# Expert loop of a mixture-of-experts block: weights split into two halves against plain f32 with the weights stationary and one ring of buffers

## The chip, the cores and the metric

The kernel runs on one core of one Trainium2 chip. The metric is the device time of the core in microseconds (us); less is better. The kernel before has a median of 4677.69 us over three runs.

## The reference, cut to what matters

The program computes two transformer blocks. The change touches one part of the first, the expert-choice feed-forward: each of 16 experts takes its 64 tokens of 512 (`cap` = 2 x 512 / 16), with D = 1024 and an inner width F = 2048, in float32.

```python
def expert_choice_ffn(h, w_router, w_gate, w_up, w_down):
    B, N, D = h.shape
    cap = EC_FACTOR * N // N_EXPERTS
    aff = jax.nn.softmax((h @ w_router).astype(F32), axis=-1)
    gate, idx = lax.top_k(jnp.swapaxes(aff, 1, 2), cap)
    xg = jax.vmap(lambda hb, ib: hb[ib])(h, idx)
    hid = jax.nn.silu(jnp.einsum('becd,edf->becf', xg, w_gate)) * jnp.einsum('becd,edf->becf', xg, w_up)
    y = jnp.einsum('becf,efd->becd', hid, w_down) * gate[..., None].astype(h.dtype)
    return jax.vmap(lambda yb, ib: jnp.zeros((N, D), yb.dtype).at[ib.reshape(-1)].add(yb.reshape(-1, D)))(y, idx)
```

The three weight tensors hold 16 x 3 x 1024 x 2048 x 4 bytes = 402.65 MB, and each byte is used once.

## The kernel before, in words

The program runs its stages one after another: modulation, norm, mixers, output projection, then `route` (the router, the choice of tokens, and the chosen tokens gathered into `ex_xg`, feature-major), `weights_back` (the weighted one-hot matrices `ex_back` that carry an expert pair's rows back to the tokens), `expert_loop`, a last norm (`final_sq` and so on), and the whole second block. Only `expert_loop` and the layout of its weights change.

`expert_loop` handles the experts in pairs: 8 turns of `positions`, each of 32 positions; the first seven turns are a hardware loop over one body, the last is written out. A position handles one chunk of 128 inner features of one expert: 16 chunks an expert, 256 in all. The work of a chunk is spread over several positions (`has(LEAD)`, `has(2)`, `has(1)`, `has(0)`):

- SyncE loads a 1 MB tile of gate and up weights (`ex_gu`, L1735) and a 0.5 MB tile of down weights (`ex_d`, L1740), four buffers each.
- Each weight tile is split into two halves of type float32r, high and low, which TensorE streams faster than plain float32. ScalarE casts the high halves (L1812, L1823), VectorE subtracts for the low half of gate and up (L1876), GpSimd for that of down (L1841).
- TensorE keeps the tokens stationary (`ex_xe`, 64 tokens as high and low part, 128 columns) and streams the 256 weight columns: 16 matmuls a chunk (L1770), then two plain f32 matmuls of 128 columns that add the token halves and turn the result (`ex_raw`, L1780).
- VectorE copies `ex_raw` out of PSUM (L1882), multiplies by the SiLU that ScalarE made (L1888), and splits the product into `ex_hT` (L1892, L1894). TensorE then streams the down weights with `ex_hT` stationary: 4 matmuls of 512 columns a chunk (L1794).
- At the end of an expert the two halves of the result are added into `ex_y` (L1828, L1904). Eight plain f32 matmuls a pair (L1757) carry the rows back to the 512 tokens, and VectorE adds them to `x` (L1860).

A plain f32 matmul of the program stands in the trace as two records, each a weight load (LDWEIGHTS, "PEld") and a MATMUL; one with float32r operands stands as one. Numbers of records are halved for plain f32 wherever instructions are meant.

## Time and profile before

| what | value |
|---|---|
| median of 3 runs (lowest, highest) | 4677.69 us (4676.04, 4678.01) |
| profiled execution: span from first to last instruction | 4676.2 us |
| mean granted TensorE clock, as a share of full speed | 0.878 |
| `expert_loop`, from its first weight load issued to its last add | 1214.2 to 2631.2 us, so 1417.0 us |
| DMA over the whole span | 573.07 MB, mean 123 GB/s |

The page prints no time of the profiled execution beside its span; the span lies between the lowest run and 1.5 us under the median, so nothing of weight lies around it. Engines are PE (TensorE matmul), PEld (its weight loads), DVE (VectorE), ACT (ScalarE), POOL (GpSimd), SP (SyncE). In the views by stretch each engine has its busy time, with the number of its instructions in brackets; PEclk is the granted clock, where 1.00 is 2.4 GHz and 0.50 is 1.2 GHz. A matmul's busy time includes its way through the pipeline, so the rate of a stream is read from the distance between starts, not from the duration of a record.

### The profile page before, as it was taken

The page shows a single profiled execution, that of the slowest core. Times are in us where ns is not written, and L with a number is a line of the kernel's source. Part 1 is how long each engine was busy: PE and PEld are TensorE (multiplying, and loading weights), DVE is VectorE, ACT ScalarE, POOL GpSimd, SP SyncE. Part 2 cuts the span into 40 slices and gives each one's busy share as a digit, 9 for nine tenths or more (in the row PEclk, how much of TensorE's full clock was granted, in tenths as well). Part 3 has the DMA queues.
Part 4 walks back from the last instruction along what each step waited for, and adds up shares of the span by engine and source line. Part 5 has one row for each costly group of instructions (what it writes and reads, how often), then busy time and mean ns, then how long its engine had stood idle before and what let it go on. Part 6 is the DMA issues. An engine that isn't in the chain of part 4 may idle for free. (4 is left out here: it accounts for less than half of the span.)

```text
span 4676.2 us, 54928 instructions
## 1 busy us (share of the span) xinstructions
PE 3468.8 (74%) x18716; PEld 2774.4 (59%) x18716; DVE 2909.6 (62%) x4362; ACT 1528.0 (33%) x1968; POOL 1362.9 (29%) x512
## 2 busy tenths in 40 slices
PE   6683767876777777777777676877676987877968
PEld 3473537865565666666656345757355865766856
DVE  5224647773799998999999645349747823144441
ACT  5110421112355555555555431112013521212121
POOL 0020000001255555655555202115320033333423
PEclk9895888967899999999999888887788998988989
DMA  6110000000587887887887531000010022222322
GB/s 250 50 61 9 5 25 1 1 15 23 214 296 270 299 295 273 297 294 273 298 296 281 190 117 50 35 26 1 0 45 7 1 72 72 73 71 77 98 66 74
DMA packets 136745, 573.07 MB, mean 123 GB/s; under 512 B 12977, under 2 KB 17457, under 8 KB 103729
## 3 DMA queue, kind: packets, MB, share of 16 engines
q1 hardware_dynamic: 136528, 570.21, 34.4%
q8 instruction: 132, 2.16, 0.2%
q14 instruction: 85, 0.70, 0.0%
HBM read 568.07 MB, written 2.10 MB: 122 GB/s over the span
## 5 line engine op out<-in xcount | busy, mean ns | idle before, releaser
L1841 POOL TENSOR_TENSOR ex_d_low<-ex_d,ex_d_high 128x1024 fp32r<-128x1024 f32 x256 | 800.3, 3126 | 724.8 <-ACT ex_d_high L1823 724.8
L1770 PE MATMUL psum<-ex_gu_high,ex_xe 128*128 128x256 f32 x2048 | 560.0, 308 | 371.6 <-DVE ex_gu_low L1876 367.3
L1770 PEld LDWEIGHTS psum<-ex_gu_high,ex_xe 128*128 128x128 f32 x2048 | 417.2, 204 | 497.5 <-DVE ex_gu_low L1876 424.2
L1876 DVE TENSOR_TENSOR ex_gu_low<-ex_gu,ex_gu_high 128x2048 fp32r<-128x2048 f32 x256 | 620.5, 2424 | 63.0 <-ACT ex_gu_high L1812 51.3
L1770 PE MATMUL psum<-ex_gu_low,ex_xe 128*128 128x256 f32 x2048 | 535.0, 295 | 0.0
L1812 ACT CAST ex_gu_high<-ex_gu 128x2048 fp32r<-128x2048 f32 x256 | 486.7, 1901 | 9.7 <-DMA ex_gu<-in_w_gate_up 5.8
L1770 PEld LDWEIGHTS psum<-ex_gu_low,ex_xe 128*128 128x128 f32 x2048 | 418.7, 204 | 0.9
L1892 DVE CAST ex_hT<-ex_hid 128x64 fp32r<-128x64 f32 x256 | 400.8, 1565 | 8.9
L466 POOL TENSOR_TENSOR out_w_low<-out_w,out_w_high 128x1024 fp32r<-128x1024 f32 x16 | 39.3, 2463 | 786.6 <-ACT out_w_high L431 786.6
L1823 ACT CAST ex_d_high<-ex_d 128x1024 fp32r<-128x1024 f32 x256 | 266.1, 1040 | 2.7 <-PE psum L1794 2.4
L1794 PE MATMUL psum<-ex_d_high,ex_hT 128*128 128x512 f32 x512 | 229.7, 449 | 12.4 <-POOL ex_d_low L1841 9.8
L1818 ACT ACTIVATE ex_sg<-psum 128x64 f32<-128x64 f32 x256 | 57.3, 224 | 539.3 <-PE psum L1780 539.1
L1794 PE MATMUL psum<-ex_d_low,ex_hT 128*128 128x512 f32 x512 | 206.3, 403 | 0.0
L1780 PE MATMUL psum<-consts,ex_raw 128*128 128x128 f32 x1024 | 164.3, 285 | 0.0
L466 POOL TENSOR_TENSOR ff_up_w_low<-ff_up_w,ff_up_w_high 128x1024 fp32r<-128x1024 f32 x44 | 105.8, 2405 | 170.6 <-ACT ff_up_w_high L431 170.6
L403 PE MATMUL psum<-ff_h_high,ff_up_w_high 128*128 128x512 f32 x352 | 138.3, 393 | 22.4 <-DVEq L416 22.4
L1780 PEld LDWEIGHTS psum<-consts,ex_raw 128*128 128x128 f32 x1024 | 145.6, 202 | 0.1
L403 PE MATMUL psum<-ff_h_low,ff_up_w_high 128*128 128x512 f32 x352 | 138.1, 392 | 0.0
L403 PE MATMUL psum<-ff_h_high,ff_up_w_low 128*128 128x512 f32 x352 | 137.9, 392 | 0.0
L2246 POOL TENSOR_TENSOR wc_at_sources<-ssd_masks,ssd_dts 128x512 f32<-128x512 f32 x64 | 73.1, 1169 | 215.8 <-SPq L2232 153.7
L466 POOL TENSOR_TENSOR in2x_w_low<-in2x_w,in2x_w_high 128x1024 fp32r<-128x1024 f32 x16 | 41.0, 2570 | 324.2 <-ACT in2x_w_high L431 324.2
L262 DVE TENSOR_TENSOR mod_w_low<-mod_w,mod_w_high 128x4096 fp32r<-128x4096 f32 x24 | 106.2, 4425 | 46.7 <-ACT mod_w_high L240 46.7
(552 smaller groups left out, 8331.0 us busy)
## 6 DMA issues: line engine op xcount, KB each, us to landing
ex_gu<-in_w_gate_up SPq DMA_DIRECT2D x256, 1024.0 KB, 6.6
ex_d<-in_w_down SPq DMA_DIRECT2D x256, 512.0 KB, 5.7
mod_w<-in_w_mod SPq DMA_DIRECT2D x24, 2048.0 KB, 9.2
ff_up_w<-in_w_up SPq DMA_DIRECT2D x44, 512.0 KB, 3.5
ff_down_w<-in_w_down SPq DMA_DIRECT2D x16, 704.0 KB, 4.0
out_w<-in_w_out SPq DMA_DIRECT2D x16, 512.0 KB, 3.4
in2x_w<-in_w_in_x SPq DMA_DIRECT2D x16, 512.0 KB, 3.2
in2z_w<-in_w_in_z SPq DMA_DIRECT2D x16, 512.0 KB, 3.3
```

The lines of the kernel that those rows point to most:

```text
L262: v.tensor_tensor(wlo[j][:, :, :], wbuf[j][:, :, :], whi[j][:, :, :], ALU.subtract).then_inc(s["low"], 1)
L403: ins = pe.matmul(banks(tile, streams)[s], weights[:, t, :], rhs(of, at), start=at == 0 and m == 0, stop=at == kt - 1 and m == len(parts) - 1)
L466: pool.tensor_tensor(wlo[b][:, :, :], wbuf[b][:, :, :], whi[b][:, :, :], ALU.subtract).then_inc(w_low[b], 1)
L1770: ins = pe.matmul(k.bank(c % 2, 2 * P), xe[:, (c // NCH) % 2, t, :, :].rearrange("p a c -> p (a c)"), w, start=t == 0 and p_ == 0, stop=t ...
L1780: ins = pe.matmul(k.psum[:, fold_bank(c), part * P:(part + 1) * P], raw[:, c % 2, part * P:(part + 1) * P], k.const("fold"), start=True, s ...
L1794: ins = pe.matmul(k.bank(4 + 2 * o + m), hT[:, b, :, :].rearrange("p a c -> p (a c)"), w, start=q % NCH == 0 and p_ == 0, stop=q % NCH == ...
L1812: act.copy(gu_hi[:, c % 2, :, :], gu[:, b, :, :]).then_inc(s["up_high"], 1)
L1823: act.copy(dw_hi[:, q % 2, :], dw[:, b, :]).then_inc(s["down_high"], 1)
L1841: pool.tensor_tensor(dw_lo[:, q % 2, :], dw[:, b, :], dw_hi[:, q % 2, :], ALU.subtract).then_inc(s["down_low"], 1)
L1876: v.tensor_tensor(gu_lo[:, c % 2, :, :], gu[:, b, :, :], gu_hi[:, c % 2, :, :], ALU.subtract).then_inc(s["up_low"], 1)
L1892: v.tensor_copy(hT[:, b, 0, :], hid[:, :]).then_inc(s["hidden_step"], 1)
L2246: pool.tensor_tensor(at_sources[:, j, :, :], masks[:, 2 + r, :].unsqueeze(1).to_broadcast([P, HALF, P]), decays.unsqueeze(2).to_broadcast( ...
```

## The change

`expert_loop` no longer splits anything. An expert has four groups (`j // 4` is the expert, 64 groups in all), each of 4 chunks of 128 inner features. A group uses three slots of one ring of seven 2 MB buffers (`ex_ring`): two with gate and up weights, one with down weights; the host lays the weights out so that a slot is one contiguous load with 16 KB a partition. A slot is loaded when the slot seven before it has been used up (`used` counts them in order). In `up` the weights are the stationary operand (128 x 128) and the 64 tokens of the expert the moving one: 32 plain f32 matmuls a slot, 64 a group, with the result inner-feature-major, as `down` wants it. ScalarE takes the SiLU of 256 columns at once, VectorE multiplies once, and nothing is turned, folded or copied. In `down` the hidden rows are stationary (64 columns) and 512 columns of weights stream: 8 plain f32 matmuls a group, whose result goes to PSUM rows 0 to 63 or 64 to 127 (`own`). After a pair, ScalarE copies both banks to `ex_y`, and eight `combine` matmuls follow, two a group, from `ex_back` itself. TensorE's order is up(j), down(j-1), combines. GpSimd does nothing here, and all loops are written out.

```diff
--- before.py
+++ after.py
@@ -1687,227 +1687,121 @@
 def expert_loop(k, xg, back):
     nc, d = k.nc, k.dram
...
-    B = 4
-    LEAD = 3
...
-        gu = k.sb("ex_gu", [P, B, KT, 2 * P], tmp)
-        dw = k.sb("ex_d", [P, B, D], tmp)
-        gu_hi, gu_lo = (k.sb(f"ex_gu_{part}", [P, 2, KT, 2 * P], tmp, R) for part in ("high", "low"))
-        dw_hi, dw_lo = (k.sb(f"ex_d_{part}", [P, 2, D], tmp, R) for part in ("high", "low"))
-        xe = k.sb("ex_xe", [P, 2, KT, 2, CAP], tmp, R)
-        raw = k.sb("ex_raw", [P, 2, 2 * P], tmp)
...
-        hT = k.sb("ex_hT", [P, B, 2, CAP], tmp, R)
-        half = k.sb("ex_half", [P, 2, 512], tmp)
+    GROUPS, G, RING = E * 4, F // 4 // P, 7
+    PAIRS = E // 2
+    up_slot = lambda j, h: 3 * j + h - (1 if j else 0)
+    down_slot = lambda j: 3 * j + 4 if j < GROUPS - 1 else 3 * GROUPS - 1
+    loaded = [k.sem(f"ex_loaded{b}") for b in range(RING)]
+    used, gated, hidden = k.sem("ex_used"), k.sem("ex_gated"), k.sem("ex_hidden")
+    y_copied, combined, x_added = k.sem("ex_y_copied"), k.sem("ex_combined"), k.sem("ex_x_added")
+    combines = {j: [] for j in range(GROUPS + 1)}
+    for i in range(PAIRS):
+        for f in range(KT):
+            combines[min(8 * i + 9 + f // 2, GROUPS)].append((i, f))
+    with ExitStack() as tmp:
+        ring = k.sb("ex_ring", [P, RING, 4096], tmp)
+        sg = k.sb("ex_sg", [P, 2, G * CAP], tmp)
+        hT = k.sb("ex_hT", [P, 3, G, CAP], tmp)
         y = k.sb("ex_y", [P, D], tmp)
-        back_now = k.sb("ex_back_now", [P, S], tmp)
         gate = k.mod1[:, 40:48, 0]
...
+        at = lambda n: ring[:, n % RING, :]
         with nc.Block() as block:
             @block.sync
             def _(sp):
...
-                positions(sp, TURNS, Q, LEAD, position)
+                def load(n, of):
+                    if n >= RING:
+                        sp.wait_ge(used, n - RING + 1)
+                    sp.dma_start(at(n), of).then_inc(loaded[n % RING], 16)
+                for j in range(GROUPS + 1):
+                    if j < GROUPS:
+                        for h in range(2):
+                            load(up_slot(j, h), d["w_gate_up"][2 * j + h, :, :])
+                    if j:
+                        load(down_slot(j - 1), d["w_down"][j - 1, :, :])
             @block.tensor
             def _(pe):
...
+                def arrived(n):
+                    pe.wait_ge(loaded[n % RING], 16 * (n // RING) + 16)
+                def up(j, h):
+                    n, e = up_slot(j, h), j // 4
+                    w = at(n).rearrange("p (c t a f) -> p c t a f", c=2, t=KT, a=2)
+                    arrived(n)
+                    for c in range(2):
+                        for a in range(2):
+                            col = a * G * CAP + (2 * h + c) * CAP
+                            for t in range(KT):
+                                ins = pe.matmul(k.psum[:, j % 2, col:col + CAP], w[:, c, t, a, :],
+                                                xg[:, t, e * CAP:(e + 1) * CAP], start=t == 0, stop=t == KT - 1)
+                    ins.then_inc(used, 1)
+                def down(j):
+                    n, e = down_slot(j), j // 4
+                    w = at(n).rearrange("p (c m) -> p c m", c=G)
+                    own = slice(CAP * (e % 2), CAP * (e % 2) + CAP)
+                    if j % 8 == 0 and e >= 4:
+                        pe.wait_ge(y_copied, e // 2 - 1)
+                    arrived(n)
+                    pe.wait_ge(hidden, j + 1)
+                    for c in range(G):
+                        for m in range(2):
+                            ins = pe.matmul(k.psum[own, 4 + 2 * (e // 2 % 2) + m, :], hT[:, j % 3, c, :],
+                                            w[:, c, m * 512:(m + 1) * 512],
+                                            start=j % 4 == 0 and c == 0, stop=j % 4 == 3 and c == G - 1)
+                    ins.then_inc(used, 1)
                 def combine(i, f):
...
+                    n = i * KT + f
+                    pe.wait_ge(y_copied, i + 1)
+                    if n >= 2:
+                        pe.wait_ge(x_added, n - 1)
+                    pe.matmul(k.bank(2 + f % 2), y[:, f * P:(f + 1) * P], back[:, i + 1, :],
+                              start=True, stop=True).then_inc(combined, 1)
+                for j in range(GROUPS + 1):
+                    if j < GROUPS:
+                        if j >= 2:
+                            pe.wait_ge(hidden, j - 1)
+                        for h in range(2):
+                            up(j, h)
+                    if j:
+                        down(j - 1)
+                    for i, f in combines[j]:
+                        combine(i, f)
             @block.scalar
             def _(act):
...
-                        act.copy(gu_hi[:, c % 2, :, :], gu[:, b, :, :]).then_inc(s["up_high"], 1)
...
-                        act.copy(dw_hi[:, q % 2, :], dw[:, b, :]).then_inc(s["down_high"], 1)
...
-                        pool.tensor_tensor(dw_lo[:, q % 2, :], dw[:, b, :], dw_hi[:, q % 2, :], ALU.subtract).then_inc(s["down_low"], 1)
...
+                for j in range(GROUPS + 1):
+                    if j < GROUPS:
+                        act.wait_ge(used, up_slot(j, 1) + 1)
+                        if j >= 2:
+                            act.wait_ge(hidden, j - 1)
+                        act.activation(sg[:, j % 2, :], k.psum[:, j % 2, 0:G * CAP], ACT.Silu).then_inc(gated, 1)
+                    if j and j % 8 == 0:
+                        i = j // 8 - 1
+                        act.wait_ge(used, down_slot(j - 1) + 1)
+                        if i:
+                            act.wait_ge(combined, KT * i)
+                        for m in range(2):
+                            ins = act.copy(y[:, m * 512:(m + 1) * 512], k.bank(4 + 2 * (i % 2) + m))
+                        ins.then_inc(y_copied, 1)
             @block.vector
             def _(v):
...
-                        v.tensor_tensor(gu_lo[:, c % 2, :, :], gu[:, b, :, :], gu_hi[:, c % 2, :, :], ALU.subtract).then_inc(s["up_low"], 1)
...
+                for j in range(GROUPS + 1):
+                    if j < GROUPS:
+                        v.wait_ge(gated, j + 1)
+                        if j >= 3:
+                            v.wait_ge(used, down_slot(j - 3) + 1)
+                        v.tensor_tensor(hT[:, j % 3, :, :].rearrange("p c n -> p (c n)"), sg[:, j % 2, :],
+                                        k.psum[:, j % 2, G * CAP:2 * G * CAP], ALU.mult).then_inc(hidden, 1)
+                    for i, f in combines[j]:
+                        v.wait_ge(combined, i * KT + f + 1)
+                        v.scalar_tensor_tensor(k.x[:, f, :], k.bank(2 + f % 2), gate[:, f:f + 1], k.x[:, f, :],
+                                               ALU.mult, ALU.add).then_inc(x_added, 1)
 def weights_back(k, aff, slot, back):
@@ -1947,9 +1841,9 @@
 def more_layout(g, out):
     out["w_router"] = g["w_router"][0]
-    tiles = [g[n][0].reshape(E, KT, P, F // P, 1, P).transpose(0, 3, 2, 1, 4, 5) for n in ("w_gate", "w_up")]
-    out["w_gate_up"] = np.concatenate(tiles, 4).reshape(E * F // P, P, KT * 2 * P)
-    out["w_down"] = g["w_down"][0].reshape(E * F // P, P, D)
+    tiles = [g[n][0].reshape(E, KT, P, F // P // 2, 2, 1, P).transpose(0, 3, 2, 4, 1, 5, 6) for n in ("w_gate", "w_up")]
+    out["w_gate_up"] = np.concatenate(tiles, 5).reshape(E * F // P // 2, P, 4096)
+    out["w_down"] = np.ascontiguousarray(g["w_down"][0].reshape(E * 4, 4, P, D).transpose(0, 2, 1, 3)).reshape(E * 4, P, 4096)
     second_layout(g, out)
```

## Rows read from the trace of the kernel before

**Rows 1.** The page: span, and busy time and share of each engine.

```profile
span 4676.2 us, 54928 instructions
...
PE 3468.8 (74%) x18716; PEld 2774.4 (59%) x18716; DVE 2909.6 (62%) x4362; ACT 1528.0 (33%) x1968; POOL 1362.9 (29%) x512
```

**Rows 2.** Stretches of the expert loop: length, busy engines, clock, DMA share, GB/s.

```profile
1400.00:1410.30 10.30, 1.57 (x10) 1.05 (x8) 6.15 (x6) 5.81 (x6) 2.57 (x2) 0.83 0.37 144
...
1500.00:1600.00 100.00, 72.93 (x457) 63.07 (x456) 90.90 (x98) 55.92 (x59) 56.14 (x20) 0.92 0.83 294
```

**Rows 3.** Groups by line, loop stretch: VectorE's two costliest, TensorE's up matmuls.

```profile
L1876 DVE TENSOR_TENSOR ex_gu_low<-ex_gu,ex_gu_high 128x2048 fp32r<-128x2048 f32 x256 | 620.5, 2424 | 63.0 <-ACT ex_gu_high L1812 51.3 <-issue 11.8
L1892 DVE CAST ex_hT<-ex_hid 128x64 fp32r<-128x64 f32 x256 | 400.8, 1565 | 8.9
...
L1770 PE MATMUL psum<-ex_gu_high,ex_xe 128*128 128x256 f32 x2048 | 560.0, 308 | 371.6 <-DVE ex_gu_low L1876 367.3 <-issue 4.3
```

**Rows 4.** Waits in the loop: total us, times, longest.

```profile
PE psum L1770 <- DVE ex_gu_low L1876: 367.3, 227, 10.2
```

**Rows 5.** Timeline at the loop's two ends: start, duration, instruction.

```profile
1211.32 0.59 ACT L1944 COPY ex_back<-psum 128x512 f32<-128x512 f32 x1 [0.27 <-PE psum L1936]
...
1214.17 2.00 SPq L1735 DMA_DIRECT2D ex_gu<-in_w_gate_up  x4
...
1218.99 1.90 ACT L1812 CAST ex_gu_high<-ex_gu 128x2048 fp32r<-128x2048 f32 x1 [5.16 <-DMA ex_gu<-in_w_gate_up]
...
2628.45 0.75 DVE L1860 SCALAR_TENSOR_TENSOR x<-psum,mod,x 128x512 f32<-128x512 f32 x1
...
2629.58 1.65 DVE L1860 SCALAR_TENSOR_TENSOR x<-psum,mod,x 128x512 f32<-128x512 f32 x2 [0.38 <-PE psum L1757]
```

**Rows 6.** Second block, timeline of TensorE: short plain f32 records; then clock by stretch.

```profile
3272.20 3.65 PE L2276 MATMUL psum<-ssd_x_lat,wc_wt 128*128 128x64 f32 x16 [3.86 <-DVE wc_wt L2306]
...
3276.17 5.95 PE L2264 MATMUL psum<-ssd_masks,wc_at_sources 128*128 128x128 f32 x32
3281.95 1.90 PE L2276 MATMUL psum<-ssd_x_lat,wc_wt 128*128 128x64 f32 x16
...
3283.96 3.74 PE L2264 MATMUL psum<-ssd_masks,wc_at_sources 128*128 128x128 f32 x32
3287.53 1.90 PE L2276 MATMUL psum<-ssd_x_lat,wc_wt 128*128 128x64 f32 x16
...
3272.30:3275.60 3.30, 3.30 (x16) 0.50 0.00 0
3284.00:3287.50 3.50, 3.50 (x34) 1.00 0.00 0
```

**Rows 7.** Long runs of short plain f32 records: timeline, then stretches with clock.

```profile
421.97 27.56 PE L718 MATMUL psum<-na_rpb,na_shift 31*128 31x60 f32 x128 [41.98 <-DMA na_mask<-in_na_mask]
...
1122.50:1135.90 13.40, 13.40 (x63) 13.40 (x64) 0.52 (x3) 1.09 (x6) 0.00 (x0) 0.50 0.00 0
421.90:449.50 27.60, 27.53 (x128) 27.38 (x128) 11.62 (x56) 0.00 (x0) 0.00 (x0) 0.50 0.00 1
```

**Rows 8.** Timeline: weight loads of a plain f32 stream of 512 columns.

```profile
2636.19 0.19 PEld L310 LDWEIGHTS psum<-final_sq,consts 128*128 128x128 f32 x1 [0.24 <-issue]
2636.62 0.19 PEld L310 LDWEIGHTS psum<-final_sq,consts 128*128 128x128 f32 x1 [0.24 <-issue]
```

**Rows 9.** Timeline: stationary operand of 128, of 64, of 128 columns.

```profile
770.26 1.10 PE L1027 MATMUL psum<-dn_vb,dn_XT 128*128 128x64 f32 x8 [0.17 <-DVE dn_XT L1094]
771.30 0.66 PE L1030 MATMUL psum<-dn_XT,dn_kbe 128*64 128x128 f32 x8
771.89 0.55 PE L1027 MATMUL psum<-dn_vb,dn_XT 128*128 128x64 f32 x3
```

**Rows 10.** Stretches with a backlog of loads, and amid the loop: DMA share, GB/s.

```profile
1216.00:1220.00 4.00, 0.00 (x0) 0.00 (x0) 0.73 (x2) 1.01 (x1) 0.00 (x0) 0.50 0.98 412
...
1516.00:1532.00 16.00, 12.32 (x83) 10.24 (x81) 15.76 (x18) 9.85 (x11) 9.50 (x4) 1.00 0.92 319
```

More of the change, by code:

```diff
@@ L1745, in _ @@
             @block.tensor
             def _(pe):
-                pe.sem_inc(s["up_done"], 2)
-                pe.sem_inc(s["down_done"], B)
-                pe.sem_inc(s["folded"], 2)
-                pe.sem_inc(s["combined"], 1)
-                def combine(i, f):
-                    pe.wait_ge(s["back_ready"], i + 1)
-                    pe.wait_ge(s["y_added"], i * 2 + 2)
-                    pe.wait_ge(s["x_added"], i * KT + f + 1)
-                    pe.matmul(k.bank(6 + f % 2), y[:, f * P:(f + 1) * P], back_now[:, :],
-                              start=True, stop=True).then_inc(s["combined"], 1)
@@ L1800, in _ @@
-                positions(pe, TURNS, Q, LEAD, position)
-                for f in range(KT):
-                    combine(TURNS, f)
+                def arrived(n):
[11 more added lines that the diff above has]
+                    ins.then_inc(used, 1)
@@ L1804, in _ @@
             @block.scalar
             def _(act):
-                def position(i, q, has):
-                    if has(LEAD):
-                        c = q + LEAD
-                        n, b = i * Q + c, c % B
-                        act.wait_ge(gu_loaded[b], (i * (Q // B) + c // B + 1) * 16)
-                        act.wait_ge(s["up_done"], n + 1)
-                        act.copy(gu_hi[:, c % 2, :, :], gu[:, b, :, :]).then_inc(s["up_high"], 1)
-                    if has(1):
-                        c = q + 1
-                        n = i * Q + c
-                        act.wait_ge(s["folded"], n + 3)
-                        act.wait_ge(s["hidden"], n + 1)
-                        act.activation(sg[:, c % 2, :], k.psum[:, fold_bank(c), 0:CAP], ACT.Silu).then_inc(s["gated"], 1)
-                    if has(0):
-                        n, b, o = i * Q + q, q % B, q // NCH
-                        act.wait_ge(d_loaded[b], (i * (Q // B) + q // B + 1) * 16)
-                        act.wait_ge(s["down_done"], n + B - 1)
-                        act.copy(dw_hi[:, q % 2, :], dw[:, b, :]).then_inc(s["down_high"], 1)
-                        if q % NCH == NCH - 1:
-                            own, other = (slice(CAP * a, CAP * a + CAP) for a in (o, 1 - o))
-                            act.wait_ge(s["down_done"], n + 1 + B)
-                            for m in range(2):
-                                ins = act.copy(half[own, m, :], k.psum[other, 4 + 2 * o + m, :])
-                            ins.then_inc(s["y_half_copied"], 1)
@@ L1831, in _ @@
-                positions(act, TURNS, Q, LEAD, position)
-            @block.gpsimd
-            def _(pool):
-                pool.sem_inc(s["down_low"], B)
-                def position(i, q, has):
-                    if has(0):
-                        n, b = i * Q + q, q % B
-                        pool.wait_ge(s["down_high"], n + 1)
-                        pool.tensor_tensor(dw_lo[:, q % 2, :], dw[:, b, :], dw_hi[:, q % 2, :], ALU.subtract).then_inc(s["down_low"], 1)
-                positions(pool, TURNS, Q, LEAD, position)
+                for j in range(GROUPS + 1):
[12 more added lines that the diff above has]
+                        ins.then_inc(y_copied, 1)
@@ L1845, in _ @@
             @block.vector
             def _(v):
-                v.sem_inc(s["up_low"], B)
-                v.sem_inc(s["up_copied"], 2)
-                v.sem_inc(s["hidden"], 2)
-                v.sem_inc(s["y_added"], 2)
-                v.sem_inc(s["x_added"], 2)
-                v.memset(y[:, :], 0.0)
-                def next_back(i):
-                    v.wait_ge(s["combined"], i * KT + 1)
-                    v.tensor_copy(back_now[:, :], back[:, bass.ds(i, 1), :].rearrange("p a n -> p (a n)")).then_inc(s["back_ready"], 1)
@@ L1907, in _ @@
-                positions(v, TURNS, Q, LEAD, position)
-                next_back(TURNS)
-                for f in range(KT):
-                    add(TURNS, f)
+                for j in range(GROUPS + 1):
[9 more added lines that the diff above has]
+                                               ALU.mult, ALU.add).then_inc(x_added, 1)
```

109 lines of the change are left out of this document (removed).

## The prediction, made before the changed kernel was run

> **What bounds the kernel now.** The page first: TensorE is busy for 74% of the span and VectorE for 62% [rows 1], an average over stages with different limits, so it decides nothing. The stretches come next. Inside the expert loop VectorE is busy for 90.9% of the time, TensorE for 73%, and the DMA engines for 83% [rows 2]. The groups say with what: the subtraction that makes the low half of the gate and up weights costs VectorE 2.42 us a chunk, and a cast of a mere 64 columns 1.57 us; TensorE's up matmuls stand idle for 371.6 us [rows 3], and 367.3 us of that end when VectorE's subtraction does [rows 4]. So VectorE, splitting weights, sets the pace. At a loop turn there is also a hole: in one stretch of 10.3 us TensorE is busy for 1.57 us [rows 2]. The loop runs from 1214.17 to 2629.58 + 1.65 = 2631.23 us [rows 5], 1417.1 us.
>
> **What the change removes.** All the splitting, on VectorE, ScalarE and GpSimd, the fold, the copies and the loop turns. VectorE keeps 64 multiplications of 256 columns and 64 adds of about 0.75 us [rows 5], under 100 us in all; ScalarE keeps 64 activations and 16 copies. Neither can bound 1400 us. TensorE and the DMA remain. TensorE gives up float32r for plain f32, which counts two records a matmul, and its order up(j), down(j-1) leaves a whole up stage to hide the SiLU and the product of group j-1. So the new loop is the length of TensorE's own stream, if the weights arrive.
>
> **The DMA.** With a backlog the queue moves 412 GB/s at a share of 0.98; amid the loop it moves 319 at 0.92, 347 at a full share [rows 10]. The 402.65 MB take 977 us by the first rate, 1160 by the second. Both lie well under the TensorE stream below, and the ring holds two groups. I cost loads at nothing; the stream covers them.
>
> **The up matmuls.** 4096 matmuls, 8192 records, each with a fresh 128-column weight load and 64 columns of tokens. The second block has this very shape, L2276. At the high clock (share 1.00) 32 records of 128 moving columns take 3287.53 - 3283.96 = 3.57 us, 0.112 us each. Sixteen of 64 columns take 1.90 us from the first start to the last end; less the last record, 3.74 - 31 x 0.112 = 0.27 us, that is 1.63 over 15 distances, 0.109 [rows 6]. Half the columns save almost nothing, so the weight load sets the rate and not the tokens. The 64-column burst has foreign neighbours that may shorten its first distance; the long run is closer to 128 records back to back, and I take 0.112. Bounds: 0.109 from below, and above it I have no row at the high clock. 8192 x 0.112 = 917.5 us (892.9 by the lower).
>
> The Trainium skill has a price for this, in "TensorE: Matmul & The Clock Gate", section "LDWEIGHTS (loading the stationary operand)": columns divided by 1.2 in ns, 107 ns for 128 columns. By it the up stages would take 8192 x 0.1067 = 874 us, 43 us less; the rows show 0.112 and decide.
>
> **The down matmuls.** 512 matmuls, 1024 records of 512 columns. Two weight loads of such a stream start 0.43 us apart [rows 8], so 440.3 us. The 64 combines (128 records) cost the same each: 55.0 us. That the stationary side of down has only 64 columns shortens a load that the long stream hides anyway.
>
> **The change of shape.** Going from a 128-column to a 64-column stationary operand is not free. A burst of L1027 starts at 770.26, its last record at 770.26 + 1.10 - 0.27 = 771.09, and L1030, with 64 stationary columns, starts at 771.30: 0.21 us later, where 0.112 is the usual distance. On the way back it is 771.30 + 0.66 - 0.27 = 771.69 to 771.89, 0.20 [rows 9]. About 0.10 us extra each way, twice a group: 128 x 0.10 = 12.8 us. Bound from below: nothing, if the long down records hide it.
>
> **The cold start.** Before the loop TensorE waits for its first weights, and at 1216 to 1220 the clock is at its low level, 0.50 [rows 10]. Does a stream of short records raise it? In 27.6 us of 60-column records without a gap it stayed at 0.50, and so it did in the router's 13.4 us [rows 7]. The 64-column burst at the low clock took 3.65 us, (3.65 - 0.42) / 15 = 0.215 a record [rows 6]; the long run (27.56 - 0.42) / 127 = 0.2137 [rows 7]. The first two groups' up stages, 256 records, run before the first down. I take them all at the low clock: 256 x (0.2137 - 0.112) = 26.0 us. The down stage then lets the clock rise with a delay: in the second block 32 denser records took 3281.95 - 3276.17 = 5.78 us instead of 3.57 [rows 6], so 2.2 us more. From then on TensorE never waits, and I keep it at the high level; the present loop, with TensorE idle for a quarter of the time, already has 0.92 [rows 2].
>
> The Trainium skill says otherwise of the start: in "TensorE: Matmul & The Clock Gate", Part 1, the low level is that of an idle engine and sustained matmuls end it. By that the 28 us would not be paid. The 27.6 us run speaks against it here, though it used only 31 rows of the array.
>
> **Start and tail.** The first load now is 2 MB instead of 1. 1 MB was there 4.8 us after its issue [rows 5]; the second takes 2.5 us at 412 GB/s [rows 10]: 7.3 us from 1214.17 to the first matmul. At the end ScalarE copies both banks, 0.27 + 2 x 0.59 = 1.4 us [rows 5], before the last eight combines, which VectorE's adds space out by about 0.1 us each (0.7), and the last add ends about 1.0 after its matmul. 3.1 us. The satisfied waits between slots cost nothing: the run of 32 in rows 6 contains such waits, one to every eight records.
>
> **The sum.** 7.3 + 917.5 + 440.3 + 55.0 + 12.8 + 26.0 + 2.2 + 3.1 = 1464.2 us, against 1417.1 now: 47.1 more. Against the span of 4676.2 that is 4723.3; the median of the runs lies 1.5 above that span, so 4724.8 us. The saved work was on other engines; the price is on the one that now decides.
>
> **Rivals.**
> *The clock is high from the start.* For it: nothing but that the 27.6 us run fills fewer rows. 28.2 us less, 4696.6. Chance 0.08. The page named above gives the same.
> *A record costs exactly half of what it costs at the low clock,* 0.2137 / 2 = 0.1069, since the low-clock rate scales with the clock. Against it: both high-clock bursts show more. 8192 x 0.0051 = 42 us less, 4683, no change. Chance 0.06.
> *The faster side: the weight load hides behind the record before.* Then a 64-column record costs an eighth of a 512-column one, 0.054, the up stages 440 us, and the DMA becomes the bound with 1160 us: 4724.8 - (1464 - 1180), 4441. Against it: 64 and 128 columns cost nearly the same [rows 6]. It decides from 57 us less on, that is at 0.105 us a record, under every row. Chance 0.04.
> *The clock falls in up stages.* If a short stall lets it drop, the short records don't raise it again before the next down: 128 x 0.102 + 2.2 = 15.2 us a group. One group in ten makes 97 us, 4822; every group 973, 5698. Against it: nothing in the order waits. Chance 0.07.
> *The DMA starves TensorE* with 16 KB a partition in a row; it would have to stay under 402.65 / 1464, 275 GB/s, below what the loop has now, 294 [rows 2]. At 250 it gives 1611 us, 4872. Chance 0.03.
>
> **How the numbers follow.** The forecast holds 0.72: 4725, with its own range from 4700 (0.109 a record; free changes of shape alone give 4712) to 4745, for small stalls that no row prices. The range for 8 in 10 reaches down to the clock's rival and up by as much: 4690 to 4755; the half-clock rival, the faster one and the two slow ones stay outside, 0.20. What a measurement of this kernel can tell from no change is about 0.2%, 9.4 us. Slower: 0.72 + 0.08 + 0.07 + 0.03 = 0.90, less a little for a start and a rate that err together, 0.88. Same: 0.07. Faster: 0.05.
>
> **What would show it.** In the profile after: VectorE under 10% busy in the loop and TensorE near 100%; up records 0.112 us apart and down records 0.43; clock 0.50 in the first two groups, then 1.00; SyncE waiting for `used`, TensorE never for a DMA; a DMA rate near 285 GB/s. A group should take 128 x 0.112 + 16 x 0.43 + 0.2 = 21.4 us. The prediction falls if the clock shows 0.50 later on, if the up records stand at another distance, or if TensorE waits for weights.

## The result, and the profile after

| kernel | median us (lowest to highest) | profiled execution: span us, mean clock |
|---|---|---|
| before | 4677.85 (4676.04 to 4679.27) | 4676.2, 0.878 |
| changed | 4723.65 (4720.69 to 4728.78) | 4721.5, 0.895 (its own time 4723.34) |

The kernel before was run again beside each set of experiments, with medians from 4676.5 to 4677.4; the ratios below are against these. The ratio here is 1.0100 with a 95% interval of 1.0087 to 1.0114: the changed kernel is slower by 1.0%, 45.8 us, well outside the 0.2% that the forecast took for no change. The forecast was 4725, with 4690 to 4755.

The page of the changed kernel shows the trade at once; beside it stand [rows 1].

```profile
PE 3890.0 (82%) x21772; PEld 3018.8 (64%) x21772; DVE 1703.0 (36%) x3064; ACT 785.1 (17%) x1248; POOL 562.3 (12%) x256
...
PEclk9895978967699999999999988887788998988989
DMA  6110000000587777777777351100010022222322
```

VectorE lost 1207 us of work and ScalarE 743, and the time grew by 46. TensorE's busy time grew by 421 us. The view by stretches shows where the bound went; [rows 2] are its counterpart (busy time and number for PE, PEld, DVE, ACT and POOL, then clock, DMA share and GB/s).

```profile
1222.00:1277.00 55.00, 54.70 (x256) 54.69 (x256) 0.42 (x1) 0.38 (x1) 0.00 (x0) 0.50 0.80 335
...
1300.00:1600.00 300.00, 300.00 (x1971) 226.65 (x1970) 11.92 (x22) 6.44 (x16) 0.00 (x0) 1.00 0.79 287
```

TensorE is busy for 300.00 of 300 us, VectorE for 4%, and the DMA engines still have a fifth to spare. The first line is the cold start: the mean clock is 0.50 over the whole of it.

TensorE's timeline of the changed kernel gives every term of the sum. It stands beside [rows 5, 6, 8]; its weight loads begin at 1214.24 and its last add ends at 2678.96 + 1.61 = 2680.57, a loop of 1466.3 us.

```profile
1222.30 54.88 PE L1737 MATMUL psum<-ex_xg,ex_ring 128*128 128x64 f32 x256 [8.99 <-DMA ex_ring<-in_w_gate_up]
1277.10 8.86 PE L1751 MATMUL psum<-ex_ring,ex_hT 128*64 128x512 f32 x16
1285.89 14.51 PE L1737 MATMUL psum<-ex_xg,ex_ring 128*128 128x64 f32 x128
1300.33 7.08 PE L1751 MATMUL psum<-ex_ring,ex_hT 128*64 128x512 f32 x16
1307.34 14.51 PE L1737 MATMUL psum<-ex_xg,ex_ring 128*128 128x64 f32 x128
...
1214.24 2.05 SPq L1715 DMA_DIRECT2D ex_ring<-in_w_gate_up  x4
...
2678.96 1.61 DVE L1803 SCALAR_TENSOR_TENSOR x<-psum,mod,x 128x512 f32<-128x512 f32 x2 [0.42 <-PE psum L1761]
```

Read the starts: first up stages 54.80 us, first down 8.79, then 14.44 and 7.01 in turn, 21.45 a group; no line after the first has an idle time in brackets. The waits of the changed kernel say who is held now; [rows 4] had TensorE waiting for VectorE.

```profile
PE psum L1737 <- DMA ex_ring<-in_w_gate_up: 9.0, 1, 9.0
...
SPq L1715 <- PE psum L1737: 931.2, 124, 18.4
SPq L1715 <- PE psum L1751: 408.5, 61, 8.4
```

TensorE waits for weights once, for the first slot, and the queue of loads waits for TensorE.

### The profile page after: what moved, and what is told of

Its sections match the earlier page's. It is cut to its first block and busy times, and to the rows that moved or that the text cites. A ratio compares the mean times of both kernels' runs of the same rounds, so it can differ in the third digit from the quotient of the medians.

```text
span 4721.5 us, 53754 instructions
## 1 busy us (share of the span) xinstructions
PE 3890.0 (82%) x21772; PEld 3018.8 (64%) x21772; DVE 1703.0 (36%) x3064; ACT 785.1 (17%) x1248; POOL 562.3 (12%) x256
## 5 line engine op out<-in xcount | busy, mean ns | idle before, releaser
L1737 PEld LDWEIGHTS psum<-ex_xg,ex_ring 128*128 128x128 f32 x8192 | 947.9, 197 | 50.2 <-issue 40.9
L1737 PE MATMUL psum<-ex_xg,ex_ring 128*128 128x64 f32 x8192 | 951.3, 280 | 9.0 <-DMA ex_ring<-in_w_gate_up 9.0
L1751 PE MATMUL psum<-ex_ring,ex_hT 128*64 128x512 f32 x1024 | 454.7, 597 | 0.0
L1751 PEld LDWEIGHTS psum<-ex_ring,ex_hT 128*64 128x64 f32 x1024 | 135.7, 137 | 267.8 <-issue 263.6
L1782 ACT ACTIVATE ex_sg<-psum 128x256 f32<-128x256 f32 x64 | 24.5, 383 | 1363.1 <-PE psum L1737 1363.1
L217 PE MATMUL psum<-mod_w_high,mod_c 128*4 128x512 f32 x192 | 78.8, 410 | 67.0 <-DVE mod_w_low L262 67.0
L2194 DVE SCALAR_TENSOR_TENSOR wc_wt<-wc_wt,ssd_dts,wc_gram 128x128 f32<-128x128 f32 x256 | 123.4, 557 | 3.4 <-ACT wc_wt L2223 2.8
L403 PE MATMUL psum<-ssd_h_high,in2x_w_high 128*128 128x256 f32 (+1 forms) x256 | 88.9, 347 | 30.1 <-DVEq L416 30.1
L403 PE MATMUL psum<-ff_a_high,ff_down_w_high 128*128 128x512 f32 x176 | 69.9, 397 | 43.1 <-DVEq L416 43.1
L240 ACT CAST mod_w_high<-mod_w 128x4096 fp32r<-128x4096 f32 x24 | 86.8, 3615 | 62.6 <-DMA mod_w<-in_w_mod 62.6
L403 PE MATMUL psum<-h,in2bc_w 128*128 128x256 f32 (+1 forms) x256 | 84.3, 493 | 5.2 <-DMA in2bc_w<-in_w_in_bc 5.2
```

The lines of the kernel that those rows point to most:

```text
L217: ins = pe.matmul(k.bank(j, N, 4), c[:, t, :, :].rearrange("p a s -> p (a s)"), x[:, t, :], start=t == 0 and part == 0, stop=t == KT - 1 a ...
L240: act.copy(whi[j][:, :, :], wbuf[j][:, :, :]).then_inc(s["high"], 1)
L403: ins = pe.matmul(banks(tile, streams)[s], weights[:, t, :], rhs(of, at), start=at == 0 and m == 0, stop=at == kt - 1 and m == len(parts) - 1)
L1737: ins = pe.matmul(k.psum[:, j % 2, col:col + CAP], w[:, c, t, a, :], xg[:, t, e * CAP:(e + 1) * CAP], start=t == 0, stop=t == KT - 1)
L1751: ins = pe.matmul(k.psum[own, 4 + 2 * (e // 2 % 2) + m, :], hT[:, j % 3, c, :], w[:, c, m * 512:(m + 1) * 512], start=j % 4 == 0 and c == ...
L1782: act.activation(sg[:, j % 2, :], k.psum[:, j % 2, 0:G * CAP], ACT.Silu).then_inc(gated, 1)
```

## The experiments

**The theory** is that of the forecast: the new loop is exactly TensorE's stream, an up record costs a 128-column weight load and not its 64 tokens, the start is paid at the low clock, and a change between 128 and 64 stationary columns costs about 0.1 us. **Rivals:** the tokens have a share in the distance; the low clock at the start has another cause; the loads hold something back. The loop times below run from the first load issued to the last add, in the one execution of each kernel that was profiled. Outside the loop these executions took between 3253 and 3262 us, so a difference of a few us there says nothing.

### e1_warm: TensorE busy before the first weights

```diff
+                for _ in range(7):
+                    pe.matmul(k.bank(7), k.const("ones"), k.x[:, 0, :], start=True, stop=True)
                 for j in range(GROUPS + 1):
```

> The changed kernel with seven plain f32 matmuls of 512 columns (constants times x, result never read) put ahead of the first wait for weights, so that TensorE is busy when the first slot lands. If the low clock at the start is a matter of what TensorE did before, and the short records keep the high clock once it is there: the first two up stages take 2 x 14.4 us instead of 54.9, the first down 7.0 instead of 8.8, together 28 us less, 4696 us. Rival: the short records cannot hold the high clock without down stages between them, and it falls within the first 29 us: between 0 and 15 us less. Rival: the low clock belongs to the start of the loop itself (first loads at full rate): nothing changes, 4724 us.

Measured: median 4696.24, ratio to before 1.0069 (1.0035 to 1.0102); span 4694.4 against 4721.5; loop 1438.1 against 1466.3, 28.2 us less. But the five executions fall into two groups: 4691.54, 4695.76 and 4696.24, with a mean clock of 0.900 to 0.903, and 4725.95 and 4726.00, both at 0.897. The last two show no gain, and neither was profiled. The timeline of the profiled one (4696.24), then two stretches with TensorE alone (busy time, granted clock, DMA share, GB/s), the first of them the idle wait:

```profile
1211.04 6.25 PE L1765 MATMUL psum<-x,consts 128*128 128x512 f32 x14 [0.98 <-PEq L1815]
1218.72 28.80 PE L1737 MATMUL psum<-ex_xg,ex_ring 128*128 128x64 f32 x256 [1.44 <-DMA ex_ring<-in_w_gate_up]
1247.45 7.08 PE L1751 MATMUL psum<-ex_ring,ex_hT 128*64 128x512 f32 x16
...
1217.30:1218.70 1.40, 0.00 (x0) 1.00 1.07 456
1219.00:1247.00 28.00, 28.00 (x253) 1.00 1.01 428
```

256 records take 28.73 us instead of 54.80: the granted clock is 1.00 (2.4 GHz) through the stretch, where the changed kernel had 0.50 (1.2 GHz) for the same records after an idle wait of 8.99 us. The changed kernel had the high clock too before that wait, and lost it while TensorE was idle:

```profile
1212.50:1215.80 3.30, 0.81 (x8) 1.00 0.42 79
1216.00:1222.00 6.00, 0.00 (x0) 0.50 0.94 390
```

In the profiled execution the 6.25 us of long matmuls fill most of the wait, the clock never falls, and the short records keep it; both rivals of this run's forecast fall there. What was different in the two executions at 4726 is open: their times and clocks are those of a low start, but no trace shows it.

### e2_wide_tokens: twice the tokens through each weight tile

```diff
-                            col = a * G * CAP + (2 * h + c) * CAP
+                            col = a * G * CAP + (2 * h + c) % 3 * CAP
+                            pair = (e // 2) * 2 * CAP
                             for t in range(KT):
-                                ins = pe.matmul(k.psum[:, j % 2, col:col + CAP], w[:, c, t, a, :],
-                                                xg[:, t, e * CAP:(e + 1) * CAP], start=t == 0, stop=t == KT - 1)
+                                ins = pe.matmul(k.psum[:, j % 2, col:col + 2 * CAP], w[:, c, t, a, :],
+                                                xg[:, t, pair:pair + 2 * CAP], start=t == 0, stop=t == KT - 1)
```

> The changed kernel with 128 token columns instead of 64 moving through each weight tile of the up stages: those of both experts of a pair. The second half of each result is surplus, and the fourth chunk's result is put where the first one's is, so the output is not the reference's. If the weight load alone sets the distance of up records: 0.112 us at the high clock as with 64, and an up stage stays at 14.4 us though it streams twice the columns. If the stream has a share in it, the distance grows towards twice, up to 14.3 us more a group, 900 in all. At the start 128-column records should raise the clock by themselves, as the second block's did, so that most of the 26 us of the first two up stages vanish: about 4700 us; if they don't, 4724.

Measured: one run of 4704.54; loop 1443.6, 22.7 us less than in the changed kernel. Its timeline, then two stretches:

```profile
1223.82 30.74 PE L1738 MATMUL psum<-ex_xg,ex_ring 128*128 128x128 f32 x256 [8.86 <-DMA ex_ring<-in_w_gate_up]
1254.49 7.08 PE L1752 MATMUL psum<-ex_ring,ex_hT 128*64 128x512 f32 x16
1261.50 14.56 PE L1738 MATMUL psum<-ex_xg,ex_ring 128*128 128x128 f32 x128
1275.99 7.08 PE L1752 MATMUL psum<-ex_ring,ex_hT 128*64 128x512 f32 x16
...
1224.00:1227.00 3.00, 3.00 (x15) 0.50 1.02 437
...
1231.00:1254.00 23.00, 23.00 (x208) 1.00 1.01 426
```

An up stage takes 1275.99 - 1261.50 = 14.49 us with twice the columns, against 14.44. The second 64 columns are free, so the columns do not set the distance. The start is different as well: the granted clock goes from 0.50 to 1.00 within the first 7 us, after the same idle wait, and the first 256 records take 30.67 us, not 54.80. That start is the whole gain of this run, and it rests on one execution.

### e3_down_128: 128 stationary columns in down as well

```diff
                     for c in range(G):
+                        two = min(c, G - 2)
                         for m in range(2):
-                            ins = pe.matmul(k.psum[own, 4 + 2 * (e // 2 % 2) + m, :], hT[:, j % 3, c, :],
+                            ins = pe.matmul(k.psum[:, 4 + 2 * (e // 2 % 2) + m, :],
+                                            hT[:, j % 3, two:two + 2, :].rearrange("p c n -> p (c n)"),
```

> The changed kernel with 128 stationary columns in the down matmuls: two chunks of hidden rows side by side (the last chunk takes the two last), results in all 128 PSUM rows, so the output is not the reference's. The number and length of the streams stays. If the change between 128 and 64 stationary columns costs 0.1 us each way: 0.2 us less a group, 12.8 in all, 4711 us, and up to down to up becomes seamless. Rival: the cost is that of going between a short and a long stream, or none: 4724 us.

Measured: median 4707.62, ratio 1.0058 (1.0041 to 1.0074); loop 1448.4, 17.9 us less, of which 0.4 is the wait for the first load (7.6 against 8.1 us). Its timeline:

```profile
1283.48 14.40 PE L1737 MATMUL psum<-ex_xg,ex_ring 128*128 128x64 f32 x128
1297.72 7.09 PE L1752 MATMUL psum<-ex_ring,ex_hT 128*128 128x512 f32 x16
1304.64 14.40 PE L1737 MATMUL psum<-ex_xg,ex_ring 128*128 128x64 f32 x128
```

An up stage takes 14.24 us instead of 14.44, a down stage 6.92 instead of 7.01: 0.29 us a group, not 0.20. The effect is there, larger than forecast. Where in the group it lies is shown by the changed kernel's groups with combines, whose stationary operand has 128 columns and which stand between down and up:

```profile
1503.78 1.98 PE L1761 MATMUL psum<-ex_back,ex_y 128*128 128x512 f32 x4
1505.61 14.40 PE L1737 MATMUL psum<-ex_xg,ex_ring 128*128 128x64 f32 x128
1519.93 7.08 PE L1751 MATMUL psum<-ex_ring,ex_hT 128*64 128x512 f32 x16
```

This up stage follows 128 columns and takes 14.32 us: the way to 64 columns costs the 0.09 over e3's 14.24. The way back costs the rest, 0.20: 0.09 ahead of the first record of 128 columns and about 0.11 behind it. The Trainium skill has a rule, in "TensorEngine Tiling (Array Packing)", section "Key Properties": changing the tiling mode drains the TensorE. The traces agree in that each change costs time, 0.09 and 0.20 us; that the time is a drain, no run shows.

### e7_ring2: two buffers instead of seven

```diff
-    GROUPS, G, RING = E * 4, F // 4 // P, 7
+    GROUPS, G, RING = E * 4, F // 4 // P, 2
```

> The changed kernel with a ring of two buffers instead of seven, so that a slot's load is issued only when TensorE starts on the slot before it and has 7.2 us to land, where such loads took 7.7 us at the median. If the loads were covered by the ring alone and a short wait lets the clock fall, with the up stages then staying at the low level until a down stage: some 15 us more a group that is hit, up to 970 in all, and stretches with clock 0.5 to 0.8 all through the loop. If a short wait leaves the clock at the high level: only the waits themselves, 192 times about 0.5 us, 100 us, 4820. If two buffers were enough: 4724.

Measured: one run of 4950.56; loop 1686.9, 220.6 us more. TensorE's waits for loads come to 72.1 us, of them 8.9 for the first slot. The rest shows in the timeline and in four stretches, the last of them the whole loop:

```profile
1316.30 7.36 PE L1737 MATMUL psum<-ex_xg,ex_ring 128*128 128x64 f32 x64 [0.36 <-DMA ex_ring<-in_w_gate_up]
...
1331.54 25.40 PE L1737 MATMUL psum<-ex_xg,ex_ring 128*128 128x64 f32 x128 [0.76 <-DMA ex_ring<-in_w_gate_up]
1356.88 9.22 PE L1751 MATMUL psum<-ex_ring,ex_hT 128*64 128x512 f32 x16
...
1404.83 13.25 PE L1737 MATMUL psum<-ex_xg,ex_ring 128*128 128x64 f32 x64 [0.54 <-DMA ex_ring<-in_w_gate_up]
...
2141.15 7.08 PE L1751 MATMUL psum<-ex_ring,ex_hT 128*64 128x512 f32 x16 [2.00 <-DMA ex_ring<-in_w_down]
...
1316.40:1323.60 7.20, 7.20 (x64) 1.00 0.76 291
1331.60:1356.80 25.20, 25.20 (x128) 0.55 0.46 167
2141.20:2148.00 6.80, 6.80 (x16) 1.00 0.63 263
1214.00:2901.00 1687.00, 1609.74 (x9344) 0.89 0.66 239
```

After a wait of 0.36 us an up half-stage still takes 7.4 us at a granted clock of 1.00. After one of 0.76 us the whole stage of 128 records takes 25.3 instead of 14.4, at 0.55; the down stage behind it takes 9.22 instead of 7.08. The length of the wait alone does not decide: one of 0.54 us was followed by a slow half-stage, one of 2.00 us ahead of a down stage left the clock at 1.00, as did the idle 1.4 us in e1. So the rival of the falling clock is real where TensorE keeps being held up, and the changed kernel is at 1.00 from 1281 us to the end of its loop, with no wait for weights; which waits let the clock fall, the runs do not say. The waits themselves are 63 us. For the other 157 there is an estimate: by the clock records of the two traces TensorE was busy at the low level for 355 us of this loop and 58 us of the changed kernel's. The 297 us more, at half the speed, are worth about 148 us, what some ten of the 64 groups would cost at the forecast's 15.2.

### e4_down_pairs: the down matmuls in both halves of the array

```diff
-                    for c in range(G):
+                    for c in range(0, G, 2):
                         for m in range(2):
-                            ins = pe.matmul(k.psum[own, 4 + 2 * (e // 2 % 2) + m, :], hT[:, j % 3, c, :],
+                            for z in range(2):
+                                ins = pe.matmul(k.psum[z * CAP:(z + 1) * CAP, 4 + 2 * (e % 2) + m, :], hT[:, j % 3, c + z, :],
...
+                            ins = act.copy(half[own, m, :], k.psum[other, 4 + 2 * (e % 2) + m, :])
...
+                            ins = v.tensor_tensor(y[own, m * 512:(m + 1) * 512], k.psum[own, 4 + 2 * (e % 2) + m, :],
+                                                  half[own, m, :], ALU.add)
```

> The changed kernel with the down matmuls in pairs: the even chunk of hidden rows sums into PSUM rows 0 to 63, the odd one into rows 64 to 127, one after the other in program order with different weight columns streaming; after each expert ScalarE copies one half over and VectorE adds it, as in the kernel before. In the second block two matmuls with 64 stationary columns in different row halves of PSUM started 6 ns apart and eight records took 0.59 us. If the two halves of the array stream at the same time here too: a down stage takes 3.5 instead of 7.0 us, 220 us less over 64, while loads need 977 to 1160 us against a stream of 1246: about 4505 us. Rival: plain f32 records of 512 columns run one after another whatever rows they write: 4724. Rival: the loads become the bound, at 285 GB/s as now: 1413 us of loop, 4670.

Measured: median 4507.97, ratio 0.9644 (0.9628 to 0.9660); loop 1249.6, 216.7 us less. Its timeline, then a stretch:

```profile
1517.35 3.65 PE L1753 MATMUL psum<-ex_ring,ex_hT 128*64 128x512 f32 x16
1520.94 14.51 PE L1739 MATMUL psum<-ex_xg,ex_ring 128*128 128x64 f32 x128
...
1300.00:2400.00 1100.00, 1100.00 (x8528) 923.10 (x8527) 84.56 (x144) 38.17 (x88) 0.00 (x0) 1.00 0.87 335
```

A down stage takes 3.59 us instead of 7.01, and 64 times the 3.42 us saved is 219 of the measured 216.7: the two halves stream at the same time. The loads now run at 335 GB/s and still hold nothing back.

### e5_up_pairs and e6_all_pairs: the up matmuls in halves too

```diff
                             for t in range(KT):
-                                ins = pe.matmul(k.psum[:, j % 2, col:col + CAP], w[:, c, t, a, :],
-                                                xg[:, t, e * CAP:(e + 1) * CAP], start=t == 0, stop=t == KT - 1)
+                                for z in range(2):
+                                    ins = pe.matmul(k.psum[64 * z:64 * z + 64, j % 2, col:col + CAP],
+                                                    w[:, c, t, a, 64 * z:64 * z + 64],
+                                                    xg[:, t, e * CAP:(e + 1) * CAP], start=t == 0, stop=t == KT - 1)
```

This is e5; e6 has this edit and that of e4.

> The changed kernel with each up matmul cut into two of 64 stationary columns, results in PSUM rows 0 to 63 and 64 to 127, same tokens streaming; twice the matmuls, same work. If the weight load sets the pace and two halves load at the same time: a pair of records takes 0.056 to 0.06 us instead of 0.112, an up stage 7 to 8 us, the loop then waits for loads at 977 to 1160 us, 4240 to 4420 in all. Rival: the halves load one after another, 2 x 0.056: no change, 4724 less the 12.8 us for changes of shape that are gone, 4711. Rival: issuing four instructions a pair of records costs more than the load: a pair takes over 0.112, slower than 4724.

> Both of the two cuts together: down in pairs of row halves and up in pairs of column halves. If both halve their stage: TensorE needs about 700 to 800 us and the loads are the bound, between 977 and 1160 us of loop: 4240 to 4420. If only the down stage gains: as the run with down pairs alone, 4505, less what changes of shape cost, 4490.

Measured: e5 median 4340.98, ratio 0.9294 (0.9270 to 0.9318), loop 1085.1; e6 median 4245.88, ratio 0.9082 (0.9062 to 0.9102), loop 988.6. The timeline of e5 in a group where nothing waits:

```profile
1530.11 7.69 PE L1738 MATMUL psum<-ex_xg,ex_ring 128*64 128x64 f32 x256
1537.63 7.03 PE L1753 MATMUL psum<-ex_ring,ex_hT 128*64 128x512 f32 x16
```

256 records of 64 stationary columns take 7.52 us, 0.059 a pair, where 128 of 128 columns took 14.44. The same weights enter in half the time, with twice the records; so the distance of an up record is neither its tokens (e2) nor a fixed price for a record, and the weight load is left. The same section of the Trainium skill says that tiles can load weights and multiply in parallel; the traces of e4 and e5 agree, with 3.59 against 7.01 us and 7.52 against 14.44. In e6 the loads have become the bound, as its stretch shows:

```profile
1220.00:2170.00 950.00, 791.75 (x17263) 597.09 (x17264) 86.66 (x149) 40.09 (x93) 0.00 (x0) 0.98 1.00 421
```

402.65 MB at 421 GB/s are 956 us, 97% of the loop.

TensorE still pauses in both, and mostly not for weights. Its waits in e5 (one line), then in e6, and the page's row of the queue that carries instructions, in the changed kernel and in e5:

```profile
PE psum L1738 <- issue: 72.4, 48, 2.2
...
PE psum L1740 <- issue: 122.0, 77, 2.8
PE psum L1740 <- DMA ex_ring<-in_w_gate_up: 35.6, 33, 8.7
...
q8 instruction: 139, 2.28, 0.2%
...
q8 instruction: 203, 3.33, 0.3%
```

"issue" means that the profile shows nothing that TensorE waited for. The packets of queue q8 hold 16 KB of instructions, and the paired up stages need 64 more of them, one a group. In e5, 46 of TensorE's 49 pauses over 0.3 us behind the start, 71 of 74 us, end 1.1 to 1.6 us after such a packet has landed, where chance would give one in sixteen; in e6 it is 78 of 116. So e5, whose loop has 83 us of idle TensorE, is held by its own stream and most likely by the arrival of its code, and not by the weights. That is read from the traces; no run tests it.

### e9_all_pairs_warm and e10_half_loads: is it the loads?

```diff
-                    sp.dma_start(at(n), of).then_inc(loaded[n % RING], 16)
+                    part = slice(0, 4096 if n < RING else 2048)
+                    sp.dma_start(at(n)[:, part], of[:, part]).then_inc(loaded[n % RING], 16)
```

This is e10, on top of e6; e9 is e6 with the seven matmuls of e1.

> The kernel with up and down stages in pairs, plus the seven plain f32 matmuls of 512 columns ahead of the first wait. If the loads bound that loop from its start to its end (they moved 424 GB/s at a share of 1.01): no change against 4246 us, since the first seven slots fill meanwhile and only their order of use moves. Rival: the slow first stages are on the path: about 15 us less, 4231.

> The kernel with up and down stages in pairs, where every load after the first seven moves only the first half of each partition's 16 KB; the other half keeps older weights, so the output is not the reference's. TensorE's work stays. If the loads are the bound: the loop shrinks from 989 us to TensorE's stream, 64 x (7.7 + 3.6) + 55 for the combines + some 35 at both ends = 813, so about 4070 us, and TensorE waits no more. Rival: TensorE's issue of 18,000 short instructions pairs holds it back: 4246 as before.

Measured: e9 median 4245.61, ratio 0.9076 (0.9061 to 0.9092), loop 987.2, no change against e6; e10 one run of 4067.43, loop 810.1. e9 says less than it seems to. In e6 there were hardly 28 us to gain: its paired up records bring the clock up by themselves, from 0.50 in the first stretch below to 1.00 in the second, and its first two up stages take 24.5 us against 22.3 in e9.

```profile
1221.00:1224.00 3.00, 3.00 (x58) 0.50 1.01 431
1228.00:1232.00 4.00, 2.54 (x88) 1.00 1.00 422
```

e10 is the test: with half the bytes the loop falls by 178 us to 810.1, where 813 was expected for TensorE's stream. e6 is bound by its loads. TensorE does still pause in e10, for 23.5 us in 18 places marked "issue", each 1.1 to 1.6 us behind a packet of instructions. In e6 it was 122.0 us in 77 places. So whether the full loads of e6 hold TensorE back by late weights or by late code as well, e10 does not separate; it shows that the bytes do it.

### e8_before_half_low: the bound of the old loop

```diff
-                            for p_, w in enumerate((gu_hi[:, c % 2, t, :], gu_lo[:, c % 2, t, :])):
+                            for p_, w in enumerate((gu_hi[:, c % 2, t, :], gu_lo[:, c % 2, t % 4, :])):
...
-                        v.tensor_tensor(gu_lo[:, c % 2, :, :], gu[:, b, :, :], gu_hi[:, c % 2, :, :], ALU.subtract).then_inc(s["up_low"], 1)
+                        v.tensor_tensor(gu_lo[:, c % 2, 0:4, :], gu[:, b, 0:4, :], gu_hi[:, c % 2, 0:4, :], ALU.subtract).then_inc(s["up_low"], 1)
```

> The kernel before, where VectorE makes the low half of the gate and up weights for only four of the eight feature tiles of a chunk, and TensorE uses these four twice; the low parts of the other four are left out, so the output is not the reference's. TensorE's matmuls, ScalarE's casts and all loads stay. If VectorE sets the pace of the old loop: half of 2.42 us less a chunk, up to 256 x 1.2 = 310 us, less what the next engine or the loads hold back (the loads need 977 to 1160 us of the 1417): between 4370 and 4550 us. Rival: TensorE or the loads set the pace: 4677 us.

Measured: one run of 4468.10; loop 1205.5 against 1417.1. A stretch of it, and VectorE's two costliest groups, beside [rows 3]:

```profile
1500.00:1600.00 100.00, 85.38 (x525) 70.86 (x525) 85.59 (x121) 63.05 (x65) 53.76 (x22) 0.95 0.90 340
...
L1892 DVE CAST ex_hT<-ex_hid 128x64 fp32r<-128x64 f32 x256 | 434.9, 1699 | 8.9
L1876 DVE TENSOR_TENSOR ex_gu_low<-ex_gu,ex_gu_high 128x1024 fp32r<-128x1024 f32 x256 | 345.7, 1350 | 73.1 <-ACT ex_gu_high L1812 62.1 <-issue 11.0
```

Taking work from VectorE alone gives 212 us: it set the pace of the old loop. It did not give the whole 310. The subtraction fell by 275 us (620.5 to 345.7), and the cast at L1892 took back 34 (400.8 to 434.9): 241 us less work, of which 212 came through. TensorE at 85% and the loads at a share of 0.90 are close behind, as a likely reason for the rest.

## Why the prediction was right, point by point

| term | forecast us | measured us | from |
|---|---|---|---|
| start, first load to first matmul | 7.3 | 8.1 | 1222.30 - 1214.24 |
| 8192 up records | 917.5 | 911.4 | 14.24 / 128 = 0.1112, e3 |
| 1024 down records | 440.3 | 442.9 | 6.92 / 16 = 0.4325, e3 |
| combines and tail | 58.1 | 58.3 | 28 x 1.72 (e3), and 23.98 - 32 x 0.4325 from the last down on |
| changes of shape | 12.8 | 17.5 | 1466.3 - 1448.4 (e3), less 0.4 of the start |
| first two up stages at the low clock | 26.0 | 26.3 | 54.80 - 2 x 14.24 |
| first down | 2.2 | 1.8 | 8.79 - 7.01 |
| loop | 1464.2 | 1466.3 | |

**What bounds the kernel now.** That VectorE set the pace was right (e8), and so was what followed: freeing it is worth nothing if the engine behind it gets 1400 us of work. Here TensorE's plain f32 stream makes a loop 49 us longer than the old one.

**The up matmuls** were priced from a burst of the second block with the very shape. That the load and not the stream sets the distance is shown by e2 and e5; the price was 0.001 us high. The price of the Trainium skill, 107 ns, in "TensorE: Matmul & The Clock Gate", section "LDWEIGHTS (loading the stationary operand)", would have made the up stages 37 us too cheap.

**The change of shape** was mis-sized: 0.10 us each way from bursts whose streams were short, 0.29 a group in the loop. The way there was right, with 0.09; the way back from a 512-column record, for which no row stood, costs 0.20, twice as much. This error of 4.7 us, one of 2.6 in the down records and one of 0.8 in the start are offset by the 6.1 us by which the up records were too dear. That the median came out 1.2 us from the forecast is luck: single terms were off by up to 6.1 us, and the time outside the loop varies by up to 9 us between the profiled kernels.

**The cold start** was right in both parts: the 27.6 us run of 60-column records spoke truly for full rows as well, and the profiles of e3, e4 and e7 have the same 54.7 to 54.8 us. e1 shows that the same records run at the high clock if it has not fallen before them, e2 and e6 that other records (128 moving columns, or pairs of 64 stationary ones) reach it behind the same kind of wait. Without the low start the changed kernel is still slower than before: the three executions of e1 that show the gain lie 0.4% above it. The 0.7% of all five mixes in the two that do not.

**The loads** were rightly costed at nothing. That neither of the two rates was a ceiling was not seen: e6 moved 421 GB/s through 950 us, a little over the backlog's 412 and far more than the 347 worked out from the present loop.

**Rivals.** None came true. The falling clock came in e7, among some 75 waits for loads; the changed kernel waits for one load only, that of its first slot. The rival of the faster side was sought in the wrong place: behind a short record with the full 128 columns the weight load does not hide, but two loads of 64 columns run side by side in the two halves of the array (e5), a case that [rows 9] already held, in the first block, with eight records in 0.59 us.

Three remainders. Outside the loop the changed kernel's profiled execution is 4 us shorter than that of before (3255.2 against 3259.1); among the twelve profiled kernels this part runs from 3253 to 3262, so nothing hangs on it. Two of five executions of e1 do not show the gain, and no trace says why. And that the pauses of e5, e6 and e10 are waits for code was read from when they end, not tested.

## What to carry to other kernels

Ask of each matmul what its record pays for: with a fresh 128-column f32 operand and few moving columns it pays for the weight load, 0.111 us here with 64 columns as with 128, and freed engines do not help. Half-width stationary operands with results in both halves of the PSUM rows load and stream side by side: 4723.65 became 4245.88 us, until the loads from memory were the bound; doubling the number of TensorE's instructions had a price as well, 71 us of pauses in e5 at the arrival of code. Before taking work off the engine that sets the pace, add up what the change puts on the next one.

## What the runs showed of the hardware that was not expected

- Short plain f32 records (64 columns, back to back) ran at a granted clock of 0.50 for 54.8 us behind an idle wait of 9 us, and for 54.7 to 54.8 in e3, e4 and e7; but at 1.00 for 28.7 us where long matmuls had filled the wait (e1) and, with down stages between, through the rest of the loop. Records with 128 moving columns (e2), and pairs with 64 stationary columns (e6), were at 1.00 some 7 us after their start.
- The clock of the changed kernel was 1.00 from 1212.5 to 1215.8 us and 0.50 from 1216 to 1222, where TensorE was idle. In e7 a wait of 0.36 us among short records left the high clock alone and one of 0.54 was followed by a slow half-stage; yet one of 2.00 us before a down stage, and the idle 1.4 us of e1, left it at 1.00.
- Two matmuls with 64 stationary columns in different PSUM row halves cost what one costs: 3.59 against 7.01 us a down stage, 0.059 us a pair of up records, with four instructions in it.
- From 128 to 64 stationary columns costs 0.09 us, back again behind 512-column records 0.20 (e3).
- Loads of 16 KB a partition run at 421 GB/s for 950 us while TensorE is 83% busy.
- In the kernels with paired up records, TensorE's pauses end 1.1 to 1.6 us after a 16 KB packet of instructions has landed: 46 of 49 in e5, 18 of 19 in e10.
